# The first layer's input is loaded in class order, tile by tile, ahead of the weights

## The reference, cut to what matters

```python
def rms_norm(x, gain):
    xf = x.astype(jnp.float32)
    y = xf * lax.rsqrt(jnp.mean(xf * xf, axis=-1, keepdims=True) + RMS_EPS)
    return (y * gain.astype(jnp.float32)).astype(x.dtype)

h = x                                            # (1, 256, 1024)
hn = rms_norm(h, attn_norm[0])
qkv = (hn @ w_in).reshape(bsz, seq, 3, 3, 16, 64)  # 3 groups, q/k/v, 16 heads
# q, k: rms_norm with a gain per group, rope; attention within the window of
# the group at its dilation 1, 4 or 16; softmax over the groups' log sums
h = h + mix @ w_out
```

## Time and profile before

| | |
|---|---|
| three runs, us | 1834.04, 1841.0, 1843.09; median 1841.0 |
| span of the profiled execution, us | 1833.9 (first to last instruction) |
| TensorE busy | 92% |
| VectorE, ScalarE, GpSimd busy | 62%, 47%, 14% |
| bytes read from memory | 238 MB, 131 GB/s over the span |

### The profile page before, as it was taken

One profiled execution on the slowest core, in us unless ns is written; L12 is line 12 of the kernel. 1 busy time (PEld: TensorE's weight loads), 2 busy tenths in 40 slices (PEclk: granted clock), 3 DMA queues, 4 the chain that ended last, 5 costly groups with the idle time before them and its releaser, 6 DMA issues. The chain is left out here.

```text
span 1833.9 us, 25119 instructions
## 1 busy us (share of the span) xinstructions
PE 1683.5 (92%) x10106; PEld 1462.5 (80%) x10106; DVE 1135.5 (62%) x1463; ACT 867.2 (47%) x1077; POOL 250.9 (14%) x207
## 2 busy tenths in 40 slices
PE   4998999989999898889999889988989899989998
PEld 3777888879998776689988678767879878779986
DVE  3877676755554466645546774358887565567764
ACT  5444565654443374444444424364544554345552
POOL 2653340000000000000000700004453100000000
PEclk8999999998999999899999999988999999989999
DMA  5453335655555354356544413100000155445543
GB/s 206 161 177 122 125 127 162 201 165 155 185 184 167 132 184 147 110 172 187 188 158 145 138 26 116 46 18 1 1 1 2 47 185 170 159 143 182 180 161 121
DMA packets 161907, 240.97 MB, mean 131 GB/s; under 512 B 12640, under 2 KB 80992, under 8 KB 161664
## 3 DMA queue, kind: packets, MB, share of 16 engines
q1 hardware_dynamic: 154400, 232.81, 39.1%
q10 hardware_dynamic: 7104, 4.64, 0.9%
q0 software_dynamic: 288, 1.92, 0.3%
HBM read 238.29 MB, written 1.05 MB: 131 GB/s over the span
## 5 line engine op out<-in xcount | busy, mean ns | idle before, releaser
L197 DVE TENSOR_TENSOR wlo<-raw,whi 128x2048 fp32r<-128x2048 f32 x224 | 524.1, 2352 | 298.9 <-ACT whi L191 288.4
L191 ACT ACTIVATE whi<-raw 128x2048 fp32r<-128x2048 f32 x224 | 420.6, 1888 | 294.9 <-PE ps L328 250.9
L326 PE MATMUL ps<-xs,whi 128*128 128x256 f32 (+1 forms) x1312 | 387.7, 296 | 17.8 <-DVE xs L460 7.4
L327 PE MATMUL ps<-xs,whi 128*128 128x256 f32 (+1 forms) x1312 | 386.1, 294 | 0.0
L328 PE MATMUL ps<-xs,wlo 128*128 128x256 f32 (+1 forms) x1312 | 386.1, 294 | 0.0
L326 PE MATMUL ps<-whi,xs 128*128 128x512 f32 x672 | 275.5, 410 | 21.4 <-DVE wlo L197 13.0
L326 PEld LDWEIGHTS ps<-xs,whi 128*128 128x128 f32 x1312 | 250.4, 191 | 27.0 <-issue 20.5
L327 PE MATMUL ps<-wlo,xs 128*128 128x512 f32 x672 | 270.0, 402 | 0.0
L328 PE MATMUL ps<-whi,xs 128*128 128x512 f32 x672 | 269.6, 401 | 0.0
L327 PEld LDWEIGHTS ps<-xs,whi 128*128 128x128 f32 x1312 | 250.4, 191 | 5.7
L328 PEld LDWEIGHTS ps<-xs,wlo 128*128 128x128 f32 x1312 | 250.2, 191 | 5.8
(11 more groups left out here) (364 smaller groups left out, 2382.7 us busy)
## 6 DMA issues: line engine op xcount, KB each, us to landing
raw<-in_ffn_w_gate_up SPq DMA_DIRECT2D x88, 512.0 KB, 4.7
raw<-in_a_w_in SPq DMA_DIRECT2D x72, 512.0 KB, 4.6
raw<-in_w_in SPq DMA_DIRECT2D x60, 512.0 KB, 4.6
raw<-in_w_mod SPq DMA_DIRECT2D x48, 512.0 KB, 4.6
raw<-in_w_up SPq DMA_DIRECT2D x44, 512.0 KB, 4.8
raw<-in_ffn_w_down SPq DMA_DIRECT2D x40, 512.0 KB, 4.5
raw<-in_b_w_in SPq DMA_DIRECT2D x24, 512.0 KB, 4.6
raw<-in_w_down SPq DMA_DIRECT2D x20, 512.0 KB, 4.0
```

Source lines behind the costliest of these rows:

```text
L191: self.hi_ok.inc(act.activation(self.whi[:, h % NHI, 0:nk, :], self.raw[:, h % NRAW, 0:nk, :], ACT.Copy))
L197: self.lo_ok.inc(dve.tensor_tensor(self.wlo[:, h % NRAW, 0:nk, :], self.raw[:, h % NRAW, 0:nk, :], self.whi[:, h % NHI, 0:nk, :].bitcast(F ...
L326: pe.matmul(o, ahi, bhi, start=start, stop=False)
L327: pe.matmul(o, ahi, blo, start=False, stop=False)
```

## The change

`norm_split` is replaced by `first_norm`. x is now loaded straight in class order into a float32 buffer `x` in the working area, by two DMAs of 64 partitions for each tile: tile 0 from ScalarE's queue, tile 1 from SP's, ahead of all weights. The identity and the vectors follow on ScalarE's queue. Each tile has its own semaphore. ScalarE first does a root of one element, to have the table loaded, and then for each tile waits for it alone, squares and takes the root; VectorE scales each tile when its root is there; TensorE transposes tile by tile. The wait for the identity and the vectors now stands before the split on ScalarE and VectorE and before the transposes on TensorE. The split has no permutation and no staging. GpSimd issues the constants after x has landed, and then, after all engines have waited for the constants, a second DMA of x, in input order, into `resid`; VectorE waits for that one before the layer's `split_and_add`.

```diff
-    def norm_split(src, seq, c, scale, chunk, shift=None, perm=None):
-        st, sq, xn, stage = c(8), c(D), c(TT, D), c(4, 512)
-        stage_at, rt0, sc0 = Stage(), st_rt.n, st_ready.n
-        split = Split(lambda t, k: xn[:, t, k * P:(k + 1) * P], seq, stage, scale, shift, perm)
+    def first_norm(scale, chunk):
+        c = Carve()
+        x, st, sq, xn = c(TT, D), c(8), c(D), c(TT, D)
+        by_class_of = ins["x"][0].rearrange("(a b c) d -> c b a d", b=4, c=4)
+        rt0, sc0 = st_rt.n, st_ready.n
+        split = Split(lambda t, k: xn[:, t, k * P:(k + 1) * P], 0, None, scale)
+
+        def load(eng, t):
+            for j in range(2):
+                x_in[t].inc_dma(eng.dma_start(x[64 * j:64 * j + 64, t, :], by_class_of[2 * t + j]))
 
         def on_act():
-            stage_at.meet(act)
+            act.wait_ge(vs.sem, vs.n)
+            act.activation(small[:, 5:6], eps_col, ACT.Sqrt)
             for t in range(TT):
-                as_.inc(act.activation(sq, src[:, t, :], ACT.Square, scale=D ** -0.5, accum_out=st[:, t:t + 1]))
+                act.wait_ge(x_in[t].sem, 32)
+                as_.inc(act.activation(sq, x[:, t, :], ACT.Square, scale=D ** -0.5, accum_out=st[:, t:t + 1]))
                 act.wait_ge(as_.sem, as_.n)
-            st_rt.inc(act.activation(st[:, 0:TT], st[:, 0:TT], ACT.Sqrt, bias=eps_col))
+                st_rt.inc(act.activation(st[:, t:t + 1], st[:, t:t + 1], ACT.Sqrt, bias=eps_col))
             W.hi(chunk[0])
+            act.wait_ge(first_in.sem, first_in.n)
             split.on_act()
             W.hi(chunk[1])
 
         def on_dve():
-            dve.wait_ge(st_rt.sem, rt0 + 1)
-            vs.inc(dve.reciprocal(st[:, 0:TT], st[:, 0:TT]))
-            dve.wait_ge(vs.sem, vs.n)
             for t in range(TT):
-                i_ = dve.tensor_scalar(xn[:, t, :], src[:, t, :], st[:, t:t + 1], None, ALU.mult)
-            st_ready.inc(i_)
+                dve.wait_ge(st_rt.sem, rt0 + t + 1)
+                vs.inc(dve.reciprocal(st[:, t:t + 1], st[:, t:t + 1]))
+                dve.wait_ge(vs.sem, vs.n)
+                st_ready.inc(dve.tensor_scalar(xn[:, t, :], x[:, t, :], st[:, t:t + 1], None, ALU.mult))
             W.lo(chunk[0])
+            dve.wait_ge(first_in.sem, first_in.n)
             split.on_dve()
             W.lo(chunk[1])
 
         def on_pe():
-            pe.wait_ge(st_ready.sem, sc0 + 1)
-            split.on_pe()
+            pe.wait_ge(first_in.sem, first_in.n)
+            for t in range(TT):
+                pe.wait_ge(st_ready.sem, sc0 + t + 1)
+                split.tile_on_pe(t)
...
         on_pool()
+        dve.wait_ge(consts_in.sem, 32)
         split_and_add(lambda t, k: o[:, t, k * P:(k + 1) * P], 0, out_chunks, nxt, norm, perm="out")
...
-    first_in.inc_dma(act.dma_start(resid[:, :, :], ins["x"][0].rearrange("(t p) d -> p t d", p=P)))
-    first_in.inc_dma(act.dma_start(cst[:, 0:P], ins["consts"][:, 0:P]))
-    first_in.inc_dma(act.dma_start(vec[:, :], ins["vecs"]))
     vs.inc(dve.memset(small[:, :], 0.0))
     dve.wait_ge(vs.sem, vs.n)
     vs.inc(dve.memset(eps_col, EPS))
-    for e in (pe, act, dve, pool):
-        e.wait_ge(first_in.sem, first_in.n)
-    act.wait_ge(vs.sem, vs.n)
-    consts_in.inc_dma(pool.dma_start(cst[:, P:], ins["consts"][:, P:]))
...
-    norm_split(resid, 0, Carve(), a_norm[:, 0, :], N["a_in"][0], perm="in")
+    x_load, x_act, x_dve, x_pe = first_norm(a_norm[:, 0, :], N["a_in"][0])
+    x_load(act, 0)
+    x_load(sp, 1)
+    first_in.inc_dma(act.dma_start(cst[:, 0:P], ins["consts"][:, 0:P]))
+    first_in.inc_dma(act.dma_start(vec[:, :], ins["vecs"]))
+    x_act()
+    x_dve()
+    x_pe()
+    pool.wait_ge(x_in[0].sem, 32)
+    pool.wait_ge(x_in[1].sem, 32)
+    consts_in.inc_dma(pool.dma_start(cst[:, P:], ins["consts"][:, P:]))
     for e in (pe, act, dve, pool):
         e.wait_ge(consts_in.sem, consts_in.n)
+    consts_in.inc_dma(pool.dma_start(resid[:, :, :], ins["x"][0].rearrange("(t p) d -> p t d", p=P)))
     M.stationary()
```

More of the change, by code:

```diff
@@ L462, in on_dve @@
                 xs_lo.inc(i_)
-    def norm_split(src, seq, c, scale, chunk, shift=None, perm=None):
-        st, sq, xn, stage = c(8), c(D), c(TT, D), c(4, 512)
-        stage_at, rt0, sc0 = Stage(), st_rt.n, st_ready.n
-        split = Split(lambda t, k: xn[:, t, k * P:(k + 1) * P], seq, stage, scale, shift, perm)
+    nw_raw = Signal(nc, "dma", "narrow_in")
+    x_in = [rows_in, nw_raw]
+    def first_norm(scale, chunk):
[7 more added lines that the diff above has]
+                x_in[t].inc_dma(eng.dma_start(x[64 * j:64 * j + 64, t, :], by_class_of[2 * t + j]))
         def on_act():
-            stage_at.meet(act)
+            act.wait_ge(vs.sem, vs.n)
+            act.activation(small[:, 5:6], eps_col, ACT.Sqrt)
             for t in range(TT):
-                as_.inc(act.activation(sq, src[:, t, :], ACT.Square, scale=D ** -0.5, accum_out=st[:, t:t + 1]))
+                act.wait_ge(x_in[t].sem, 32)
+                as_.inc(act.activation(sq, x[:, t, :], ACT.Square, scale=D ** -0.5, accum_out=st[:, t:t + 1]))
                 act.wait_ge(as_.sem, as_.n)
-            st_rt.inc(act.activation(st[:, 0:TT], st[:, 0:TT], ACT.Sqrt, bias=eps_col))
+                st_rt.inc(act.activation(st[:, t:t + 1], st[:, t:t + 1], ACT.Sqrt, bias=eps_col))
             W.hi(chunk[0])
+            act.wait_ge(first_in.sem, first_in.n)
             split.on_act()
@@ L480, in on_dve @@
         def on_dve():
-            stage_at.meet(dve)
-            dve.wait_ge(st_rt.sem, rt0 + 1)
-            vs.inc(dve.reciprocal(st[:, 0:TT], st[:, 0:TT]))
-            dve.wait_ge(vs.sem, vs.n)
             for t in range(TT):
-                i_ = dve.tensor_scalar(xn[:, t, :], src[:, t, :], st[:, t:t + 1], None, ALU.mult)
-            st_ready.inc(i_)
+                dve.wait_ge(st_rt.sem, rt0 + t + 1)
+                vs.inc(dve.reciprocal(st[:, t:t + 1], st[:, t:t + 1]))
+                dve.wait_ge(vs.sem, vs.n)
+                st_ready.inc(dve.tensor_scalar(xn[:, t, :], x[:, t, :], st[:, t:t + 1], None, ALU.mult))
             W.lo(chunk[0])
+            dve.wait_ge(first_in.sem, first_in.n)
             split.on_dve()
@@ L492, in on_pe @@
         def on_pe():
-            stage_at.meet(pe)
-            pe.wait_ge(st_ready.sem, sc0 + 1)
-            split.on_pe()
-        on_act()
-        on_dve()
-        on_pe()
+            pe.wait_ge(first_in.sem, first_in.n)
+            for t in range(TT):
+                pe.wait_ge(st_ready.sem, sc0 + t + 1)
+                split.tile_on_pe(t)
+        return load, on_act, on_dve, on_pe
     tile_ok = Signal(nc, "pe", "last_tile")
@@ L608, in add_product @@
         return on_pe, on_act, on_dve
-    nw_raw, nw_hi = Signal(nc, "dma", "narrow_in"), Signal(nc, "act", "narrow_hi")
+    nw_hi = Signal(nc, "act", "narrow_hi")
     nw_lo, nw_out = Signal(nc, "dve", "narrow_lo"), Signal(nc, "pe", "narrow_out")
```

## The result

The changed kernel takes 1847.4 us (median of 6 runs, 1840.2 to 1849.9) against 1837.3 for the kernel before in the same comparison (6 runs, 1834.0 to 1843.1). The ratio is 1.0042, 95% interval 1.0024 to 1.0060: slower by 4.4 to 11 us. 1840 was predicted, with 1845 as the upper end. Runs of one kernel spread by some 10 us, and with them TensorE's mean granted clock: 1840.2 us at 0.966, 1849.9 at 0.958.

What follows compares the result with a forecast made beforehand. TensorE, busy 92% of 1833.9 us, was taken as the bound, losing time only in stops. Its first start moves 0.2 us later, its second 0.7 earlier: 1841.0 - 0.7 = 1840.3, taken as 1840, range 1831 to 1845.

Steps and rivals of the forecast that it cites:

- All four x transfers share them at 4 x 26 = 104 GB/s: 1.05 MB takes 10.1 us: Load of x at the start: four engines carry it from 2.7 to 12.8 us, landing at 14.0.
- the two queues take turns with equal packets: Load of x on ScalarE's and SP's queues: both tiles land together, at 14.0 us.
- The first square to W.hi of half 0: ScalarE's norm at the start: squares and two roots take 2.8 us, 14.0 to 16.8; W.hi waits for half 0 until 17.2.
- The split: Split without staging after the norm: 8 activations in 3.01 us, 8 subtractions in 3.23, VectorE late, TensorE starting at 25.0.
- The constants: GpSimd's constants, issued at 14.0 once x has landed: 8.3 us to land, at 22.3, covered by 1.7 us.
- the rival with the constants in the backlog: Start of the kernel: constants land at 28.9, TensorE's second start comes 3.3 us later, time 1846; chance 0.09.
- The gains: Gains' DMA before GpSimd's tables: issued at 25.7, landing at 30.6, tables 0.7 us earlier, TensorE going on at 41.7.
- The copy of x into the residual's buffer: The resid copy behind the constants: 0.7 us of issue on POOL, read at layer A's end, VectorE's added wait costing nothing.
- the rest shifts rigidly: After TensorE's second start: all that follows moves by as much as 42.45 moves, predicted 0.7 us earlier.
- 3.5 more for half 0's place behind it: First weight half behind x on SP's queue: landing at 17.2 instead of 9.1, counted as 3.5 us of added wait.
- the DMA share of the first 13 us is well under the 0.72: Sign of four engines at the start: DMA share there well below the 0.72 of the first 24.85 us before.
- The rival of sixteen engines: Load of x at the start: spread over 16 engines it lands at 6.5, 8 us gained, time 1833; chance 0.13.

Runs made afterwards that it cites:

- e7: The changed kernel, but SP issues no weight until both tiles of x have landed; ratio 1.0021 to the kernel before.
- e9: Probe on e4: the change's four 64-partition transfers, sent beside the weights into a place nobody reads; packets 280 and 165 ns, kernel time meaningless.
- e10: Probe as e9, but eight transfers of 16 rows led by four, into partitions 0 to 15; packets 164 and 87 ns, kernel time meaningless.
- e1: The changed kernel with x loaded by eight DMAs of 16 rows for each tile instead of two of 64; ratio 0.9979 to the kernel before.
- e4: The changed kernel, x in input order by one 128-row DMA a tile into the residual's buffer, class order made by transposes; median 1831.2 us, ratio 0.9949.
- e6: e2 with each DMA writing every second partition instead of the first or last 64; ratio 0.9959 to the kernel before.
- e8: e4's norm and split, but x fetched as before the change by a single DMA with the common wait; ratio 0.9985 to the kernel before.
- e2: The changed kernel with each x DMA reading 64 rows that follow each other, class order left out; ratio 0.9975 to the kernel before.
- e11: e4 with the gains' DMA issued behind the vectors at the start instead of after the split; ratio 0.9941 to the kernel before.

## Why the prediction was wrong

The direction of the mechanism was right: the four DMAs do run on four engines (e7's share of 26%), which outweighs all that the new norm gives. The wrong step is the size of one term, "All four x transfers share them at 4 x 26 = 104 GB/s: 1.05 MB takes 10.1 us". Beside the weights it is about 57 GB/s, and x landed at 21.4 instead of 14.0. Nor did the tiles land together, as "the two queues take turns with equal packets" had it: tile 1's last packet ends at 17.7, and that of tile 0, for which ScalarE waits first, at 20.3. The 26 GB/s came from a stretch in which every DMA led with 128 partitions; I carried it over to one with another shape, beside traffic of the old shape. e7, without that traffic, flows at the 102 GB/s computed; e9 shows that the mixture slows both, and e10 that the number of engines alone does not.

What stands behind that term held, moved by about the same 7.4 us:

- The first square to W.hi of half 0: 2.8 us predicted, 2.75 measured. Half 0 was not awaited further, a wait of 0.4 us that was predicted and isn't there: its second DMA, issued at 2.6, landed 21.3 us later, at 23.9, just ahead of W.hi at 24.17.
- The split: 3.0 and 3.2 us predicted, 3.03 and 3.22 measured, VectorE last. TensorE's first weight matmul was predicted 11.0 us behind x's landing, measured 10.5.
- The constants: 8.3 us predicted from issue, 8.0 measured, issued at 21.7; they landed before ScalarE's W.hi of half 1 ended at 31.3. So the rival with the constants in the backlog did not happen, although the side on which it lay was the right one.
- The gains: 4.9 us predicted to land, the tables start 4.6 after the issue. TensorE's second start: 41.7 predicted, 48.70 measured, 7.0 later, the term's excess.
- The copy of x into the residual's buffer ended no wait that TensorE felt.
- That the rest shifts rigidly: for the change it does, 5.9 us at 689 us for 6.25 at the second start. Over the kernels of the table the ratio times 1840 us follows the shift (the change +7.7 for +6.3, e1 -3.9 for -3.2, e4 -9.4 for -9.3, e6 -7.5 for -7.7, e7 +3.9 for +4.0), and e8's shift alone lies outside the interval of its ratio. That it fits so well is in part luck, with intervals 4 to 8 us wide: the traces' shifts move by up to 2.7 us between the second start and 689 us (e4 -7.8 there, e6 -10.0, e7 +1.8).

Two figures of the prediction are wrong without moving its sum. "3.5 more for half 0's place behind it" counts the wait for x twice: by its own times half 0 adds 0.4 us (16.8 to 17.2), and 3.5 is the whole delay of W.hi, 17.2 for 13.70. And chunk 0 would end at 38.6, not 38.2 (42.45 less 4.00, plus 0.2). Of its signs, "the DMA share of the first 13 us is well under the 0.72" could not have shown four engines: it was 0.74, since the weights kept the other twelve busy.

The rival of sixteen engines was priced at -8 us. e2 has the sixteen engines with its 64 neighbouring partitions and gives -5.5: it too missed that x into one half of the partitions flows at 225 GB/s. Only e6 comes near, with -7.7.

The range ended at 1845 since the slower side held one mechanism only, behind x. A term on which all else waits, and which is taken over from another shape of transfer, needs its own upper end: twice its time, 10.1 us more, would have given 1850.

## What to carry to other kernels

Before a load is cut or reordered, look at the outermost dimension of both of its patterns and at the partitions that it writes; a permutation that costs a few microseconds of copies can cost ten as a DMA pattern, most of all in front of a queue of weights. The same permutation was free in the output pattern of transposes that were there anyway. When a transfer is moved to the front, as in e11, check what stands behind it in the same flood: it can move the next landing by more than its bytes. And compare a shift of 6 us in two traces where it arises, not in their spans, which can differ by as much through the clock.

## What the runs showed of the hardware

- A DMA whose source pattern leads with four ran on four of 16 engines (26% share, 102 GB/s alone).
- Transfers led by four, with blocks of 16 or 32 partitions, beside 128-partition transfers on all engines, brought the total from about 400 to 212 to 228 GB/s and nearly doubled the packet times of both (280 ns for 159, 150 for 84); blocks of four partitions did not (413 GB/s).
- On 16 engines, 64 neighbouring partitions took 225 GB/s, every second of 128 took 406, 16 neighbouring ones 131.
- Transposes in float32 that write PSUM in a pattern of 8 by 4 by 4 took no longer: 3.68 us for 16 against 3.65.
- The gains' row, spread over all partitions by one DMA in the flood, landed after 9.0 us instead of 3.7 and held the first weights back by 1.9 us (e11).
